# Seven-product chunks in a float32 down projection: eight instead of six in its second half, its K tiles in another order

## The reference

```python
    hf = rmsnorm(x, norm_ffn[l])
    act = jax.nn.silu(jnp.einsum('bsd,df->bsf', hf, w_gate[l])) * jnp.einsum('bsd,df->bsf', hf, w_up[l])
    x = x + jnp.einsum('bsf,fd->bsd', act, w_down[l])
return rmsnorm(x, norm_final)
```

## Time and profile before

| what | us |
|---|---|
| median of 3 runs | 1692.24 (1692.17 to 1692.29) |
| the profiled execution | 1693.11 |
| its span, first to last instruction | 1691.3 |
| TensorE busy | 1675.6 |
| VectorE busy | 1445.7 |
| ScalarE busy | 918.5 |

### The profile page before, as it was taken

The page is one execution under the profiler, slowest core; times in us unless marked ns, Lnnn a source line. Parts: engine busy times, 40 slices in busy tenths (PEclk is TensorE's granted clock), DMA queues, the critical chain, the costliest instruction groups (busy, mean ns, idle before and its releaser), DMA issues.

```text
span 1691.3 us, 19896 instructions
## 1 busy us (share of the span) xinstructions
PE 1675.6 (99%) x7521; PEld 1385.2 (82%) x7521; DVE 1445.7 (85%) x1272; ACT 918.5 (54%) x795; POOL 71.0 (4%) x66
## 2 busy tenths in 40 slices
PE   9999999999999999999999999999999999999997
PEld 7888888888888888888888877888888888888886
DVE  6988557698898998888987499999999999898987
ACT  6655444455545555555544455565656555655554
POOL 1000111300000000000000010000000000230000
PEclk9999999999999999999999999999999999999999
DMA  9465555556566655555556556556666666566653
GB/s 376 155 219 199 174 183 184 185 189 235 199 216 230 220 199 199 200 198 199 197 182 219 185 166 220 201 198 198 198 198 198 199 199 201 195 201 222 222 192 108
DMA packets 124496, 340.88 MB, mean 202 GB/s; under 512 B 7436, under 2 KB 7564, under 8 KB 123784
## 3 DMA queue, kind: packets, MB, share of 16 engines
q1 hardware_dynamic: 122592, 334.68, 58.8%
q10 hardware_dynamic: 1832, 5.22, 1.0%
HBM read 333.60 MB, written 2.10 MB: 198 GB/s over the span
## 4 chain that ended last, share of the span: by engine, by line
PE 88%; DVE 7%; issue 2%; DMA 1%; ACTq 1%; ACT 1%; POOL 0%; DVEq 0%; POOLq 0%; SPq 0%
PE ps L1946 11%; PE ps L1953 11%; PE ps L1947 11%; PE ps L2249 8%; PE ps L2255 8%; PE ps L2251 8%; PE ps L2330 4%; PE ps L2331 4%; PE ps L2335 4%; PE ps L1874 4%; PE ps L1875 4%; PE ps L1883 4%; DVE w_lo L1135 2%; PE ps L1974 1%; PE ps L1975 1%
## 5 line engine op out<-in xcount | busy, mean ns | idle before, releaser
L1135 DVE TENSOR_TENSOR w_lo<-w_raw,w_hi 128x2048 fp32r<-128x2048 f32 x307 | 706.4, 2304 | 72.7 <-ACT w_hi L654 71.2
L654 ACT ACTIVATE w_hi<-w_raw 128x2048 fp32r<-128x2048 f32 (+1 forms) x311 | 588.3, 1896 | 331.6 <-issue 119.3
L1946 PE MATMUL ps<-w_hi,xT_hi 128*128 128x512 f32 x570 | 222.6, 391 | 0.4 <-DVE cb L1303 0.3
L1947 PE MATMUL ps<-w_hi,xT_lo 128*128 128x512 f32 x570 | 222.0, 390 | 0.0
L654 ACT ACTIVATE t_hi<-t_raw 128x1536 fp32r<-128x1536 f32 x56 | 83.3, 1488 | 127.4 <-PE ps L2255 87.1
L1953 PE MATMUL ps<-w_lo,xT_hi 128*128 128x512 f32 x570 | 150.6, 390 | 0.3 <-DVE w_lo L1135 0.3
L2249 PE MATMUL ps<-w_hi,fT_hi 128*128 128x512 f32 x352 | 139.4, 396 | 2.9 <-ACT w_hi L654 1.8
L2251 PE MATMUL ps<-w_hi,fT_lo 128*128 128x512 f32 x352 | 137.4, 390 | 0.0
L1946 PEld LDWEIGHTS ps<-w_hi,xT_hi 128*128 128x128 f32 x570 | 107.1, 188 | 23.3 <-DVE cb L1303 1.2
L1953 PEld LDWEIGHTS ps<-w_lo,xT_hi 128*128 128x128 f32 x570 | 106.8, 188 | 23.6 <-DVE w_lo L1135 1.6
L1947 PEld LDWEIGHTS ps<-w_hi,xT_lo 128*128 128x128 f32 x570 | 107.1, 188 | 22.0
(11 more groups left out here) (441 smaller groups left out, 3104.5 us busy)
## 6 DMA issues: line engine op xcount, KB each, us to landing
w_raw<-in_w_in SPq DMA_DIRECT2D x126, 1024.0 KB, 4.9
w_raw<-in_w_gate SPq DMA_DIRECT2D x88, 512.0 KB, 3.8
w_raw<-in_w_up SPq DMA_DIRECT2D x88, 512.0 KB, 4.6
w_raw<-in_w_down SPq DMA_DIRECT2D x44, 1024.0 KB, 5.1
w_raw<-in_w_branch_b SPq DMA_DIRECT2D x16, 1024.0 KB, 5.2
w_raw<-in_w_branch_a SPq DMA_DIRECT2D x16, 1024.0 KB, 5.1
w_raw<-in_w_out SPq DMA_DIRECT2D x16, 1024.0 KB, 5.7
late<-nat ACTq DMA_DIRECT2D x6, 448.0 KB
```

The costliest lines, as they stand in the source:

```text
L654: copy = lambda o, i, **kw: nc.scalar.activation(o, i, ACT.Copy, **kw)
L1135: V.tensor_tensor(w_lo[:, chunk.split, :], w_raw[:, chunk.raw, :], w_hi[:, chunk.split, :].bitcast(F32), ALU.subtract).then_inc(lo_split, 1)
L1946: T.matmul(ps[:, banks[name], :], tile(0, t), moving(0, u), start=begins, stop=False)
L1947: last = T.matmul(ps[:, banks[name], :], tile(1, t), moving(0, u), start=False, stop=False)
```

## The change

In the second half the seven-product chunks stand at s = 3, 5, 7, 9, 11, 13, 15 and 18, eight instead of six. They use the K tile pairs 3, 6, 9, 12, 15 and 18, whose forms exist since the first half, and the pairs 20 and 21 for the two last; so the second half takes its K tiles in the order 0, 1, 2, 3, 4, 6, 5, 9, 7, 12, 8, 15, 10, 18, 11, 20, 13, 14, 21, 16, 17, 19. GpSimd makes the forms of pairs 20 and 21 as its seventh and eighth (`DOWN_FORMS`), behind the splits of the fifth and sixth, so still in the first half; they are split at s = 15 and s = 18 of the second half. Their tiles, and `sq_y`, get other addresses. The first half has the same chunks as before.

```diff
-DOWN_S = (3, 6, 9, 12, 15, 18)
+DOWN_S = ((3, 6, 9, 12, 15, 18), (3, 5, 7, 9, 11, 13, 15, 18))
+DOWN_FORMS = DOWN_S[0] + (20, 21)
...
-        down_form_hi = at("down_form_hi", [P, 4 * ND, P], F32R, LATE_F + 4096)
-        down_form_lo = at("down_form_lo", [P, 4 * ND, P], F32R, LATE_F + AT + 4096)
+        down_form_hi, down_form_lo = ([at(f"down_form_{n}{d}", [P, 4, P], F32R, LATE_F + h * AT + 4096 + 2048 * d if d < 6
+                                          else R1 + 4096 * (d - 5) + 2048 * h) for d in range(ND)]
+                                      for h, n in enumerate(["hi", "lo"]))
...
-        sq_y = at("sq_y", [P, 2, COLS], F32, R1)
+        sq_y = at("sq_y", [P, 2, COLS], F32, R1 + 12288)
...
+        rest = [[k for k in range(DN) if k not in forms] for forms in (DOWN_S[0], DOWN_FORMS)]
+        DOWN_K = [[DOWN_FORMS[at_s.index(s)] if s in at_s else left.pop(0) for s in range(DN)]
+                  for at_s, left in zip(DOWN_S, rest)]
...
-            return c < 2 * DN and c % DN in DOWN_S
+            return c < 2 * DN and c % DN in DOWN_S[c // DN]
+
+        def forms_new(c):
+            return c < DN or down_form(c) >= len(DOWN_S[0])
...
-                k, col = c % DN * 2, c // DN * 2 * COLS
+                k, col = 2 * DOWN_K[c // DN][c % DN], c // DN * 2 * COLS
...
-                k = 2 * DOWN_S[d]
+                k = 2 * DOWN_FORMS[d]
...
-                k = c % DN * 2
+                k = 2 * DOWN_K[c // DN][c % DN]
...
-                    if c < DN:
-                        d = DOWN_S.index(c)
+                    if forms_new(c):
+                        d = down_form(c)
                         act.wait_ge(down_form_step, 3 * (d + 1))
...
-                if c == DN + DOWN_S[0]:
+                if c == DN + DOWN_S[1][0]:
                     pe.wait_ge(y_sum, MAIN_STEPS)
```

More of the change, by code:

```diff
@@ L295, in hybrid_block @@
         a_hi, a_lo = at("a_hi", [P, 2, 2, SEQ], F32R, LATE_F), at("a_lo", [P, 2, 2, SEQ], F32R, LATE_F + AT)
-        ND = len(DOWN_S)
-        down_form_hi = at("down_form_hi", [P, 4 * ND, P], F32R, LATE_F + 4096)
-        down_form_lo = at("down_form_lo", [P, 4 * ND, P], F32R, LATE_F + AT + 4096)
+        ND = len(DOWN_FORMS)
+        down_form_hi, down_form_lo = ([at(f"down_form_{n}{d}", [P, 4, P], F32R, LATE_F + h * AT + 4096 + 2048 * d if d < 6
+                                          else R1 + 4096 * (d - 5) + 2048 * h) for d in range(ND)]
+                                      for h, n in enumerate(["hi", "lo"]))
         down_form_raw = at("down_form_raw", [P, 2, 4, P], F32, R1)
-        assert 4 * ND * P * 4 <= AT - 4096
+        assert len(DOWN_S[1]) == ND == 8
         g_final = at("g_final", [P, D], F32, LATE)
         y = at("y", [P, RT, D], F32, LATE + D * 4)
-        sq_y = at("sq_y", [P, 2, COLS], F32, R1)
+        sq_y = at("sq_y", [P, 2, COLS], F32, R1 + 12288)
         CONST = Z + 2 * AT + 12288
@@ L411, in hybrid_block @@
         DN = FC // 2
-        D_LAST = DOWN_S[-1]
+        D_LAST = DOWN_S[0][-1]
+        rest = [[k for k in range(DN) if k not in forms] for forms in (DOWN_S[0], DOWN_FORMS)]
+        DOWN_K = [[DOWN_FORMS[at_s.index(s)] if s in at_s else left.pop(0) for s in range(DN)]
+                  for at_s, left in zip(DOWN_S, rest)]
         EXTRA_STEPS, MAIN_STEPS = 8, 4
@@ L418, in is_down_s, with down_form @@
         def is_down_s(c):
-            return c < 2 * DN and c % DN in DOWN_S
+            return c < 2 * DN and c % DN in DOWN_S[c // DN]
+        def down_form(c):
+            return DOWN_S[c // DN].index(c % DN)
+        def forms_new(c):
+            return c < DN or down_form(c) >= len(DOWN_S[0])
         def down_turns(c):
-            return T_FRONT + S_TURNS * FB + c // DN * ND + DOWN_S.index(c % DN)
+            return T_FRONT + S_TURNS * FB + c // DN * len(DOWN_S[0]) + down_form(c)
         def s_chunk_before(c):
-            if c == DOWN_S[0]:
+            if c == DOWN_S[0][0]:
                 return Chunk(G_FFN + LAST_S, FB - 1, 2 * BC)
-            d = DOWN_S.index(c % DN)
-            return down_chunk(c // DN * DN + DOWN_S[d - 1] if d else DN * (c // DN - 1) + D_LAST)
+            d = down_form(c)
+            return down_chunk(c // DN * DN + DOWN_S[c // DN][d - 1] if d else DN * (c // DN - 1) + D_LAST)
         def units(half):
@@ L1060, in down_split @@
                     turns = down_turns(c)
-                    if c < DN:
-                        d = DOWN_S.index(c)
+                    if forms_new(c):
+                        d = down_form(c)
                         act.wait_ge(down_form_step, 3 * (d + 1))
-                        copy(down_form_hi[:, 4 * d:4 * d + 4, :], down_form_raw[:, d % 2]).then_inc(
+                        copy(down_form_hi[d][:], down_form_raw[:, d % 2]).then_inc(
                             down_form_hi_done, 1)
@@ L1755, in down_split @@
                 if is_down_s(c):
-                    if c < DN:
-                        d = DOWN_S.index(c)
+                    if forms_new(c):
+                        d = down_form(c)
                         dve.wait_ge(down_form_hi_done, d + 1)
-                        V.tensor_tensor(down_form_lo[:, 4 * d:4 * d + 4, :], down_form_raw[:, d % 2],
-                                        down_form_hi[:, 4 * d:4 * d + 4, :].bitcast(F32),
+                        V.tensor_tensor(down_form_lo[d][:], down_form_raw[:, d % 2], down_form_hi[d][:].bitcast(F32),
                                         ALU.subtract).then_inc(down_form_lo_done, 1)
@@ L2319, in tile @@
                         return (a_hi, a_lo)[part][:, c % 2, int(name[2]) - 1, r * P:(r + 1) * P]
-                    n = 4 * DOWN_S.index(c % DN) + ("D1", "S1", "S2", "S4").index(name)
-                    return (down_form_hi, down_form_lo)[part][:, n, :]
+                    return (down_form_hi, down_form_lo)[part][down_form(c)][:, ("D1", "S1", "S2", "S4").index(name), :]
                 def moving(half, u):
@@ L2347, in down @@
                 if is_down_s(c):
-                    pe.wait_ge(down_form_lo_done, DOWN_S.index(s) + 1)
+                    pe.wait_ge(down_form_lo_done, down_form(c) + 1)
                     pe.wait_ge(t_hi_done, down_turns(c) + 1)
@@ L2352, in down @@
                     name = part[0]
-                    last = high(part, start=name not in begun and s == (DOWN_S[0] if name in EXTRA else 0))
+                    last = high(part, start=name not in begun and s == (DOWN_S[g][0] if name in EXTRA else 0))
                     begun.add(name)
```

## The result

| | us |
|---|---|
| before, median of 8 runs | 1692.38 (1692.17 to 1693.03) |
| changed, median of 8 runs | 1697.16 (1696.84 to 1697.95) |
| ratio | 1.0028, 95% interval 1.0019 to 1.0037 |

The changed kernel is slower by 4.8 us (by the ratio's interval, 3.2 to 6.3). The forecast was 1696.2 with a range of 1694.9 to 1697.6, so the time lies inside it, 1 us above the forecast and above the 1695.5 to 1696.9 that had the chance of 0.75.

What follows compares the result with a forecast made beforehand. TensorE, busy 99% of the span, was taken to bound the kernel. A saving of 1.36 us and waits of 5.3 gave +3.9 us on the median of 1692.24: 1696.2, range 1694.9 to 1697.6.

Steps and rivals of the forecast that it cites:

- The saving: Last projection, second half: two chunks go from 24 matmuls to 21, taking 1.36 us off PE.
- First pass: From the end of chunk 3 to chunk 6: 12.0 us where PE wants 10.20, so PE waits 1.8.
- E + 8.75: When `w_lo` of chunk 5 is ready, about 8.75 us after E, the end of chunk 3; wanted at 8.61.
- The loop: Sums, `t_hi`, `w_hi` and `a_hi`, `a_lo`, `t_lo`, `w_lo` on DVE and ACT: 11.04 us per pair, 0.84 over PE's 10.20.
- Its partner through PE: Path alternating with the DVE and ACT chain: two rounds 22.2 us against 22.08, up to 0.3 us more loss.
- Where it stops: Behind chunk 14, at chunks 16, 17 and 19: no further loss but no slack; taken as 0.
- Rival (b): Waits go on behind chunk 14, or links with PE take 0.1 more: 1 to 2 us on top; chance 0.10.
- First half: Two more forms on POOL stretch DVE by at most 1.6 us each, hidden by 3.8 us of PE cover.
- Clock: PE's waits, some 0.9 us in every 11, leave the granted clock at the 2.4 GHz level; priced at 0.
- Rival (a): ACT's part overlaps more than the chain allows, so only the saving stays: 1690.9 us; chance 0.13.

Runs made afterwards that it cites:

- `a_hi` ahead of `t_hi`: The changed kernel, with ScalarE staging `a_hi` before `t_hi` where the seven-product chunk before is two back; 1691.52 us, ratio to before 0.9995.
- the second buffer: The changed kernel, with `t_hi` of the second half going in turn to two buffers; 1694.91 us, ratio to before 1.0013.
- the longer link: The changed kernel, with ScalarE copying each `t_hi` of the second half twice; 1706.43 us, ratio to before 1.0083.
- the `a_lo` put in: The changed kernel, with VectorE making the plain chunk's `a_lo` before the weight sums between seven-product chunks two apart; 1700.12 us, ratio to before 1.0045.

## Why the prediction was right

**The saving.** Forecast 1.36 us. Six matmuls fewer in the page, and 1.36 us where nothing takes it back (`a_hi` ahead of `t_hi`).

**First pass.** Forecast 12.0 us from the end of chunk 3 to the start of chunk 6; measured 12.08. Of PE's wait 0.11 us lie before the low part of chunk 5, where I had 0.15, and by the end of that part PE is 0.24 behind. `w_lo` of chunk 5 is ready at E + 8.67, which is what its links add up to; the E + 8.75 of the prediction was a slip.

**The loop.** Forecast 11.04 us per pair, closed between VectorE and ScalarE; measured 11.02 to 11.03 with the second buffer, 12.40 with the longer link, 11.63 with the `a_lo` put in. This is the step on which the sign hangs, and four runs bear it out.

**Its partner through PE** is a term that was mis-sized. I put 0.16 us on PE's return from a wait, after the earlier trace rows, and 22.2 us on two rounds, and took 5.3 us for the whole loss. In the changed kernel `a_lo` ends at 1598.48, the first matmul starts at 1598.63 and the second 0.30 later, so 0.15 + 0.07 = 0.22. Two rounds are 22.30 us (1602.33 to 1624.63). The path through PE so bound every second round, and between chunks 4 and 14 PE lost 5.68 us (56.68 for 51.00). Part of the gap was there on paper: a first pass of 12.0 and twice 22.2 make 56.4, a loss of 5.4, and I took 5.3.

**Where it stops.** Forecast no slack and no loss at 16, 17 and 19: measured 0.03, 0.06 and 0.00 us (10.23, 5.50, 10.20 for 10.20, 5.44, 10.20). Rival (b), up to 2 us more there, did not happen; of its other form, a tenth more in each link with PE, a little did (the 0.22 for 0.16 above).

**The end of the kernel** is the term that I had not looked at: the sum has nothing for it, and it cost 0.46 us (9.60 for 9.14 behind the last two matmuls). What the runs show of it stands in the section on the result; its cause stays open. It and the 0.47 us that PE lost beyond the forecast (5.77 for 5.3) are the 1 us between forecast and time. Both errors went the same way, and the time stayed in the range thanks to the room that was left in it for rival (b), whose places lost nothing: that is luck.

**First half.** Forecast nothing. The two further forms are made at 1526.89 and 1542.41, and each stretches one `w_lo` to 2.83 us as in the earlier trace rows and the next two rows of VectorE by 0.26 us each, some 1.1 us in all where I allowed 1.6; no wait of PE, and 1692.21 us where only they and the K order are changed.

**Clock.** The granted clock is 1.00 in the stretch with the five waits (above), so PE stayed at 2.4 GHz through idle times of up to 1.39 us. The Trainium skill, "TensorE: Matmul & The Clock Gate", section "What's actually happening", says that the clock falls to half after idling; no run here shows that fall, since these waits did not set it off.

**The account.** The loss of 5.77 less 1.36 makes 4.41 us, with the 0.46 at the end 4.87; the medians differ by 4.78. In all eight kernels measured against the one before, what the traces show from chunk 2 on and at the end comes within 0.4 us of the difference of the medians. The spans are no such measure: the profiled executions differ by up to 1.8 us by the time they reach chunk 2, over stages that are the same but for the two forms. The changed kernel's was 1.09 us ahead there (`w_lo` at 1574.84 for 1575.93), which is why its span is only 3.8 us longer. Rival (a), the hidden chain, is refuted for the changed kernel, though the same work in another order (`a_hi` ahead of `t_hi`) makes it true.

## What to carry to other kernels

Before bringing two expensive steps closer together, add up the chain that leads from one to the next through all engines, in issue order, and compare it with the distance that is left; an engine's busy share cannot tell it. Where a chain closes on itself, the place of the wait is a symptom: moving the row that is waited for lengthened the loop and cost 3 us, and writing `a_hi` ahead of `t_hi`, which took `w_hi`, `a_hi` and `a_lo` out of the loop, gave back 5.6. A chain with spare distance hides 1.4 us per round entirely, the same chain without it passes nearly all of them on. And look at the end of the kernel in both traces: here half a microsecond stood in a transfer that the change did not touch.

## What the runs showed of the hardware

PE's return from a wait of 0.5 to 1.4 us cost 0.22 us beside the wait itself in these rows: 0.15 us from the end of VectorE's row to the first matmul, which takes 0.47 us in place of 0.39, and 0.07 us before the second. Beyond this nothing was unexpected.
